# Where the softmax denominators are applied in a fused two-branch attention block: on the gate path, or on the probabilities

## The reference, cut to what matters

```python
m = jnp.maximum(jnp.max(logits, axis=-1, keepdims=True), sk)            # branch A
p = jnp.exp(logits - m)
probs = p / (jnp.sum(p, axis=-1, keepdims=True) + jnp.exp(sk - m))
o = einsum(probs, vb)
probs = jax.nn.softmax(logits, axis=-1)                                 # branch B
...
ya = swa_sink_attention(qa, ka, va, a_sinks[layer]) * jax.nn.silu(za)
yb = chunked_relpos_attention(qb, kb, vb, b_rel_bias[layer]) * jax.nn.silu(zb)
merged = (jax.nn.sigmoid(ga + gate_bias[layer, 0]) * einsum(ya, w_br_a[layer])
          + jax.nn.sigmoid(gb + gate_bias[layer, 1]) * einsum(yb, w_br_b[layer]))
return rms_norm(x + einsum(merged, w_out[layer]), final_g)
```

## Time and profile before

| | |
|---|---|
| median of 3 runs | 3304.91 us (3304.08 to 3306.46) |
| profiled execution: its own time | 3306.4 us |
| profiled execution: span of the trace | 3304.6 us |
| TensorE busy | 3247.2 us (98%) |
| GpSimd, ScalarE, VectorE busy | 1457.4, 1397.8, 1366.8 us (44, 42, 41%) |
| granted TensorE clock | 0.998 of full speed |

### The profile page before, as it was taken

One profiled execution on the slowest core, in us unless ns is written; L12 is line 12 of the kernel. 1 busy time (PEld: TensorE's weight loads), 2 busy tenths in 40 slices (PEclk: granted clock), 3 DMA queues, 4 the chain that ended last, 5 costly groups with the idle time before them and its releaser, 6 DMA issues.

```text
span 3304.6 us, 48009 instructions
## 1 busy us (share of the span) xinstructions
PE 3247.2 (98%) x16248; PEld 2491.4 (75%) x16248; DVE 1366.8 (41%) x2936; ACT 1397.8 (42%) x2929; POOL 1457.4 (44%) x1216
## 2 busy tenths in 40 slices
PE   7999999999999999999999999999999999999998
PEld 6777877778777787777877778777787777877776
DVE  3562345513455134551345513455134551345512
ACT  3543344433444334453344534444344443444432
POOL 5434463344633445334453344533445334553244
PEclk9999999999999999999999999999999999999999
DMA  4222432225322243122431224322253122432123
GB/s 162 66 65 90 172 105 60 65 83 173 107 59 65 87 168 111 59 65 84 168 110 60 64 84 173 105 60 64 86 173 103 60 64 90 172 99 60 58 90 115
DMA packets 100218, 322.25 MB, mean 98 GB/s; under 512 B 11248, under 2 KB 27760, under 8 KB 97776
## 3 DMA queue, kind: packets, MB, share of 16 engines
q1 hardware_dynamic: 99952, 318.90, 29.9%
HBM read 299.45 MB, written 16.78 MB: 96 GB/s over the span
## 4 chain that ended last, share of the span: by engine, by line
PE 92%; DVE 3%; issue 2%; ACT 1%; DMA 1%; POOL 0%; ACTq 0%; SPq 0%; DVEq 0%; POOLq 0%
PE acc L947 16%; PE acc L949 16%; PE acc L948 15%; PE ps_o L1042 6%; PE ps_pt L1011 6%; PE sc L991 4%; PE sc L947 4%; PE sc L949 4%; PE sc L948 4%; PE sc L982 2%; PE sc L891 2%; PE sc L889 2%; PE sc L890 2%; PE sc L914 1%; PE acc L1051 1%
## 5 line engine op out<-in xcount | busy, mean ns | idle before, releaser
L770 POOL TENSOR_TENSOR w_lo<-w_raw,w_hi 128x512 fp32r<-128x512 f32 x928 | 1199.2, 1299 | 1766.2 <-ACT w_hi L1090 1765.4
L947 PE MATMUL acc<-h_hi,w_hi 128*128 128x512 f32 x2432 | 1007.7, 414 | 0.0
L949 PE MATMUL acc<-h_hi,w_lo 128*128 128x512 f32 x2432 | 952.6, 392 | 0.0
L948 PE MATMUL acc<-h_lo,w_hi 128*128 128x512 f32 x2432 | 949.6, 390 | 0.0
L1090 ACT ACTIVATE w_hi<-w_raw 128x512 fp32r<-128x512 f32 x928 | 577.3, 625 | 426.0 <-DMA w_raw<-w 119.5
L947 PEld LDWEIGHTS acc<-h_hi,w_hi 128*128 128x128 f32 x2432 | 457.1, 188 | 130.7 <-issue 56.3
L949 PEld LDWEIGHTS acc<-h_hi,w_lo 128*128 128x128 f32 x2432 | 456.4, 188 | 101.2
L948 PEld LDWEIGHTS acc<-h_lo,w_hi 128*128 128x128 f32 x2432 | 458.8, 189 | 74.5
L1178 ACT ACTIVATE probs_b<-sc,negm 128x640 f32<-128x640 f32 x256 | 203.6, 796 | 372.0 <-DVE negm L1294 371.3
L1185 ACT ACTIVATE probs_t<-ps_pt 128x512 f32<-128x512 f32 (+1 forms) x272 | 154.5, 568 | 333.2 <-PE ps_pt L1011 333.2
L1319 DVE SCALAR_TENSOR_TENSOR part<-th,sc 128x512 f32<-128x512 f32 x64 | 43.9, 686 | 449.1 <-PE sc L949 449.1
(11 more groups left out here) (135 smaller groups left out, 3884.3 us busy)
## 6 DMA issues: line engine op xcount, KB each, us to landing
w_raw<-w SPq DMA_DIRECT2D x464, 512.0 KB, 3.5
rows<-x SPq DMA_DIRECT2D x36, 512.0 KB, 7.7
xt<-x_t SPq DMA_DIRECT2D x16, 1024.0 KB, 9.3
out<-rows SPq DMA_DIRECT2D x32, 512.0 KB, 2.8
x_in<-x SPq DMA_DIRECT2D x28, 512.0 KB, 5.4
cs<-rope_tab SPq DMA_DIRECT2D x8, 512.0 KB, 4.3
rot<-pre SPq DMA_DIRECT2D x160, 16.0 KB
bias<-near SPq DMA_DIRECT2D x1, 1024.0 KB, 13.6
```

What stands on the lines that cost most here:

```text
L770: pool.tensor_tensor(w_lo[n % 2][:, c], w_raw[n % 2][:, c], w_hi[n % 2][:, c].bitcast(FP32), ALU.subtract).then_inc(w_split, 1)
L947: pe.matmul(dst[:, :], hi, src_hi[:, k, :], start=begin, stop=False)
L948: pe.matmul(dst[:, :], hi, src_lo[:, k, :], start=False, stop=False)
L949: mm = pe.matmul(dst[:, :], lo, src_hi[:, k, :], start=False, stop=end)
```

## The change

The denominators move from the gate path to the probabilities.

- A new step `scale` follows each `exps` in the list. GpSimd waits for the exponentials of one query tile (both heads). For an A set it adds exp(sink - max) to the two sums. It raises the sums to the power -1 and multiplies the two tiles of probabilities in place with the result. Turns wait for this (`probs_scaled`) and no longer for the exponentials.
- exp(sink - max) is made by ScalarE one column at a time, just ahead of the exponential of the same head and query tile: 256 instructions in A sets instead of 64.
- `D` and `norm` are gone: no reciprocal and no spreading on DVE, no four transposes and no product `gate` for each of the 64 sets, and no `acc` bank taken for it.
- `ps_o` is cleared by a DVE memset, once a block behind the B values' copies and after each `gate` but the last, and all value matmuls accumulate. The first values of a set wait for the memset (`o_zeroed`) instead of for L1378.
- With no group to start, the turns of B sets come in another order: key tile -3 first, which needs query tiles 0 and 1 alone, then -2, -1, 0, 1, 2 and the last one. The number of transposes and value matmuls and their sizes stay.
- The factor 0.5 moves into `gate` on ScalarE and `gate_rest` on DVE.
- The weight tile `z7` comes two tiles later, and z's tanh uses another buffer.

```diff
-B_TURNS = [[(0, -1)], [(1, -1)], [(0, 0)], [(1, 0)], [(0, -2)], [(1, -2)], [(0, 1)], [(1, 1)],
-           [(0, -3), (1, -3)], [(0, 2), (1, 2)], [(0, -4), (1, -4), (0, 3), (1, 3)]]
+B_TURNS = [[(0, -3), (1, -3)], [(0, -2)], [(1, -2)], [(0, -1)], [(1, -1)], [(0, 0)], [(1, 0)], [(0, 1)],
+           [(1, 1)], [(0, 2), (1, 2)], [(0, -4), (1, -4), (0, 3), (1, 3)]]
-B_BURSTS = [[-1], [0], [-2], [1], [-3], [2], [-4, 3]]
+B_BURSTS = [[-3], [-2], [-1], [0], [1], [2], [-4, 3]]
-B_OUT = (1, 0, 0, 1, 0, 0, 1, 1, 0, 0, 0)
+B_OUT = (1, 0, 0, 1, 0, 0, 1, 0, 0, 1, 0)
...
-A_BEATS = "T0 F G T1 F H D T2 V0 V1 S0 F E0 T3 F F S1 V2 V3 F E1 F S2 F E2 F F S3 F E3 F"
-B_BEATS = "F T0 F G T1 F H D T2 F T3 F V0 V1 S0 S1 T4 F E0 T5 F E1 T6 F T7 F V2 V3 S2 S3 T8 F E2 T9 F T10 E3 F V4 V5 V6"
+A_BEATS = "T0 F G T1 F H T2 V0 V1 S0 F E0 T3 F F S1 V2 V3 F E1 F S2 F E2 F F S3 F E3 F"
+B_BEATS = "F T0 F G T1 F H T2 F T3 F V0 V1 S0 S1 T4 F E0 T5 F E1 T6 F V2 V3 S2 S3 T7 F E2 T8 F T9 E3 F T10 F V4 V5 V6"
...
-        lead[at_] = [("scores", 0, t), *lead[at_], ("exps", 0, t)]
+        lead[at_] = [("scores", 0, t), *lead[at_], ("exps", 0, t), ("scale", 0, t)]
...
-                plan.append(("exps", nxt, no))
+                plan += [("exps", nxt, no), ("scale", nxt, no)]
...
+                    elif step[0] == "scale":
+                        s, t = step[1:]
+                        n, c = POS[s], slice(2 * t, 2 * t + 2)
+                        total = sums[:, n % 2, c]
+                        if s < PAIRS:
+                            hold(sink_exp, b * (2 * TT * PAIRS) + (2 * TT * s + 2 * t + 2))
+                            hold(probs_ready, unit(b, s, t, 1) + 1)
+                            pool.tensor_tensor(total, total, esink[:, c], ALU.add).then_inc(den_ready, 1)
+                            hold(den_ready, b * (TT * PAIRS) + (TT * s + t + 1))
+                        else:
+                            hold(probs_ready, unit(b, s, t, 1) + 1)
+                        pool.tensor_tensor(rden[:, n % 2, c], total, minus[:, :], ALU.pow).then_inc(rden_ready, 1)
+                        hold(rden_ready, tile_no(b, s, t) + 1)
+                        for hh in range(2):
+                            p_ = weights_of(s, hh, t)
+                            pool.tensor_scalar(p_, p_, rden[:, n % 2, 2 * t + hh:2 * t + hh + 1], None,
+                                               ALU.mult).then_inc(probs_scaled, 1)
...
-                pe.wait_ge(probs_ready, unit(b, s, needed - 1, 1) + 1)
+                pe.wait_ge(probs_scaled, unit(b, s, needed - 1, 1) + 1)
...
-                    if not (first and POS[s] == 0):
-                        pe.wait_ge(y_whole, b * SETS + POS[s])
+                    pe.wait_ge(o_zeroed, b * SETS + POS[s] + 1)
...
-                                       start=j == every[0], stop=j == every[-1], skip_group_check=True)
+                                       start=False, stop=j == every[-1], skip_group_check=True)
...
-                    elif kind == "norm":
-                        claim(b, step)
-                        pe.wait_ge(rows_ready, b * SETS + (POS[step[1]] + 1))
-                        turn_four(b, step, part)
...
+                            if s < PAIRS:
+                                head = head_no(s, hh)
+                                act.activation(esink[:, c:c + 1], negm[:, POS[s] % 2, c:c + 1], ACT.Exp,
+                                               bias=sink_sb[:, head:head + 1]).then_inc(sink_exp, 1)
...
-                        wait_freed(dve, b, ("norm", s))
-                        dve.tensor_tensor(whole[:, :], ps_o[:, :], gate[:, :], ALU.mult).then_inc(y_whole, 1)
+                        wait_freed(dve, b, ("job", "z", s))
+                        dve.tensor_tensor(whole[:, :], ps_o[:, :], z[POS[s] % 2][:, :], ALU.mult).then_inc(y_whole, 1)
+                        if s != ORDER[-1]:
+                            dve.wait_ge(y_whole, b * SETS + (POS[s] + 1))
+                            dve.memset(ps_o[:, :], 0.0).then_inc(o_zeroed, 1)
```

More of the change, by code:

```diff
@@ L98, in weight_tiles @@
         tiles += [("ga", d), ("gb", d)]
+        if d == 0:
+            tiles.append(("z", SETS - 1))
     for d in range(KT):
@@ L109 @@
 V_BANK = 1
+Z_TH = 2 * AHEAD - 1
 SQUARED_AT = (4, 5, 8, 10)
@@ L206, in block_plan @@
                     plan.append(("keep_v", ORDER[n - 1]))
-        assert quarters == BEATS_QUARTERS and ("norm", s) in plan
+        assert quarters == BEATS_QUARTERS
     for steps in fill:
@@ L268, in check_plan @@
     assert [step[1] for step in PLAN if step[:1] == ("mm",) and step[2] == 0] == list(range(NW))
-USES_ACC = ("job", "turn_v", "norm")
+USES_ACC = ("job", "turn_v")
 check_plan()
@@ L741, in _ @@
             pool.memset(mhalf[:, :], -0.5).then_inc(zeroed, 1)
+            pool.memset(minus[:, :], -1.0).then_inc(zeroed, 1)
             pool.memset(k_a[:, 0:P], 0.0).then_inc(zeroed, 1)
@@ L1142, in job_done @@
                 elif name == "z":
-                    act.activation(th[:, 0, :], ps, ACT.Tanh, scale=0.5).then_inc(z_tanh, 1)
+                    act.activation(th[:, Z_TH, :], ps, ACT.Tanh, scale=0.5).then_inc(z_tanh, 1)
                 elif name in ("ga", "gb"):
                     i = ("ga", "gb").index(name)
-                    if name == "ga" and idx == 0:
+                    if 2 * idx + i == Z_TH:
                         wait_freed(act, b, ("job", "z", ORDER[-1]))
@@ L1185, in body @@
                             act.activation(ring(first, turn)[:, 0:n], ps_pt[:, 0:n], ACT.Copy).then_inc(pt_out[0], 1)
-                    elif kind == "sink" and step[1] < PAIRS:
-                        s = step[1]
-                        nm = negm[:, POS[s] % 2, :].rearrange("p (t h) -> p h t", h=2)
-                        es = esink[:, :].rearrange("p (t h) -> p h t", h=2)
-                        for hh in range(2):
-                            head = head_no(s, hh)
-                            act.activation(es[:, hh, :], nm[:, hh, :], ACT.Exp,
-                                           bias=sink_sb[:, head:head + 1]).then_inc(sink_exp, 1)
                     elif kind == "gate":
@@ L1198, in body @@
                             act.wait_ge(out_sent, b * (16 * TT))
-                        act.activation(y_hi[:, s, :], whole[:, :], ACT.Copy).then_inc(y_hi_done, 1)
+                        act.activation(y_hi[:, s, :], whole[:, :], ACT.Copy, scale=0.5).then_inc(y_hi_done, 1)
                     elif kind == "next_square" and not last:
@@ L1353, in body @@
                         dve.tensor_copy(v_b[:, TT + 1, :], ps_v[1]).then_inc(v_out[1], 1)
-                    elif kind == "denominators":
-                        s = step[1]
-                        n = POS[s]
-                        dve.wait_ge(probs_ready, unit(b, s, TT - 1, 1) + 1)
-                        total = sums[:, n % 2, :]
-                        if s < PAIRS:
-                            dve.wait_ge(sink_exp, b * (2 * PAIRS) + (2 * s + 2))
-                            dve.tensor_tensor(den[:, :], total, esink[:, :], ALU.add).then_inc(den_ready, 1)
-                            dve.wait_ge(den_ready, b * PAIRS + (s + 1))
-                            total = den[:, :]
-                        dve.reciprocal(rden[:, :], total).then_inc(rden_ready, 1)
-                        dve.wait_ge(rden_ready, b * SETS + (n + 1))
-                        dve.tensor_scalar(part[:, :].rearrange("p (n c) -> p n c", c=HD),
-                                          rden[:, :].unsqueeze(2).to_broadcast([P, 2 * TT, HD]), 0.5, None,
-                                          ALU.mult).then_inc(rows_ready, 1)
-                    elif kind == "norm":
-                        s = step[1]
-                        wait_full(dve, b, step)
-                        dve.tensor_tensor(gate[:, :], bank(step)[:, :], z[POS[s] % 2][:, :],
-                                          ALU.mult).then_inc(free(step), 1)
+                        dve.wait_ge(v_out[0], 2 * (b + 1))
+                        dve.memset(ps_o[:, :], 0.0).then_inc(o_zeroed, 1)
                     elif kind == "gate":
@@ L1387, in body @@
                         dve.wait_ge(y_hi_done, b * SETS + (POS[s] + 1))
-                        dve.tensor_tensor(y_lo[:, s, :], whole[:, :], y_hi[:, s, :].bitcast(FP32),
-                                          ALU.subtract).then_inc(y_done, 1)
+                        dve.scalar_tensor_tensor(out=y_lo[:, s, :], in0=whole[:, :], scalar=0.5,
+                                                 in1=y_hi[:, s, :].bitcast(FP32),
+                                                 op0=ALU.mult, op1=ALU.subtract).then_inc(y_done, 1)
                     elif kind == "add_rows":
```

26 lines of the change are left out of this document (11 added, 15 removed).

## The result

The changed kernel takes 3549.7 us (median of 4 runs, 3547.4 to 3553.3), the kernel before 3305.3 beside it. The ratio is 1.074 (95% interval 1.072 to 1.076): 244 us slower, where 3298 us and a range up to 3330 were forecast.

The account below looks back on a forecast made before the run. The prediction took TensorE, busy 3247.2 of 3304.6 us, as the bound. From the median of 3304.9 it summed -27.5 (norms) + 5 (scores) + 15 (first sets) + 1 (ScalarE) = -6.5: 3298 us, range 3283 to 3330.

Parts of the forecast that it names:

- the price of the multiplication: On GpSimd, each multiplication of a scale: 0.40 us for 256 columns and 0.72 for 640, upper bounds 0.65 and 1.62.
- it fits: GpSimd in the steady sets: with four scales added, busy 22 of 26 us in A sets, 17 of 27 in B.
- 27.5 us from the norms: On TensorE, 64 norms of four transposes go, each costing 0.43 us: 27.5 us saved.
- 5 us for scores: In 32 A sets, scores of query tile 2 wait for exponentials, losing 0.12 to 0.19 us each: 5 us taken.
- The first set: In each block's first set, scales and low parts queue on GpSimd, delaying turns by 1.9 us: 15 us in 8 blocks.
- 2 to 4 us later: GpSimd's low parts in steady sets come 2 to 4 us later, with room in the list; no loss in the sum.
- ScalarE: One-column sink exponentials at 0.2 to 0.25 us, about 40 us more work on ScalarE; 1 us lost, up to 6.
- rival 1: In the first set a scale under 1.7 us costs turns only ScalarE's 0.5 us, 4 us: 3287 us; chance 0.2.
- VectorE: VectorE gets lighter; the new memset of some 0.5 us is hidden, with 4 us to spare before the values.
- Rival 2: GpSimd becomes the bound, multiplying at the two-input rate; first sets and B sets' turns wait: 3377 us; chance 0.25.
- Rival 3: VectorE's `y_lo` and GpSimd hold each other up, 32 us on top: 3330 us; chance 0.1, with late low parts.

Follow-up runs that it names:

- constant-factor run: The changed kernel with a constant factor of 0.125 in place of the column of reciprocals in both multiplications, output not normalised: 3524.6 us (1.067).
- copy run: The changed kernel with each multiplication replaced by a GpSimd copy of the tile onto itself, output not normalised: 3309.4 us (1.0009).
- A tiles alone: The changed kernel with full multiplications of A tiles only, one column multiplied of B tiles: 3343.3 us (1.011).
- B tiles alone: The changed kernel with full multiplications of B tiles only, one column multiplied of A tiles: 3514.1 us (1.064).
- broadcast version: The changed kernel, same result, with each multiplication written as a two-input product with the reciprocal's column broadcast along the row: 3364.6 us (1.018).

## Why the prediction was wrong

**The step that failed is the price of the multiplication**, and in it the choice of bounds. The prediction took 0.40 and 0.72 us from the copy and 0.65 and 1.62 from the subtraction as the upper end. Measured were 0.93 and 1.90. The bounds assumed that an instruction with one large input can't be dearer than one with two. The constant-factor run shows that it is: 2.5 ns a column, as much as the two-input subtraction takes if nothing of its 1299 ns is fixed, and 852 - 256 x 2.5 = 0.2 us on top, with the column of scalars 0.3. The trace of before had no such instruction of size. An upper end from the nearest row was no upper end. Nor was the lower end as firm as it looked. The prediction took the key copy of 512 columns, 613 ns; the value copy of the same size took 607 to 1087 in the same trace:

```profile
L804 POOL COPY v_b<-v_b 128x512 f32<-128x512 f32 x28 | 26.9, 959 | 0.0
```

The copies of the copy run did keep to the lower price.

The Trainium skill (GPSIMD Engine Reference, 4.1 Engine selection) has instructions with one input near line rate. By this trace the rule holds for copies and not for a multiplication by a scalar, which runs slower than a broadcast product with two inputs. The estimate from its section 3.1, 0.38 and 0.96 us, is 0.4 and 0.5 of what was measured. The measurement decides. Its advice to keep elementwise work off GpSimd was right for the B tiles.

**What the price did.** The steady sets were the prediction's "it fits": 22 of 26 us. With the measured pieces a B scale is 0.73 + 0.21 + 3.75 = 4.7 us, and an A set asks GpSimd for 12.3 + 4 x 4.7 = 31 us in 26. The runs order themselves by that sum, 12.3 + 4 x (0.93 + 2m), with m the duration of a B tile's multiplication. The fourth column is the first set's part: what has come up by the second set's first turn against the run without multiplications, in all 8 blocks. It goes mostly by the price of the A tiles (A tiles alone give 53, B tiles alone 17).

| run | m, us | GpSimd's work in an A set of 26 us | first sets, us | time, us |
|---|---|---|---|---|
| none | 0 | 16 | 0 | 3286.9 |
| copy | 0.72 | 22 | 13 | 3309.4 |
| broadcast product | 1.27 | 26 | 30 | 3364.6 |
| constant factor | 1.82 | 31 | 52 | 3524.6 |
| as changed | 1.90 | 31 | 60 | 3549.7 |

Below the edge the steady sets cost little. At it they cost some 50 us, and beyond it what GpSimd falls behind in an A set is paid in the B set behind it, and in part at half clock.

**Point by point.**

- 27.5 us from the norms, less 5 us for scores: right. Without multiplications it is 3286.9 us; the terms -27.5 + 5 + 4 + 1 gave 3287. The loss at the scores was 0.11 us a set, 3.5 us, below the 4 to 6.
- The first set: right in mechanism and, at the copy's price, in size (12 us against 15). At the true price it is some 60 of the 263 us that the multiplications cost, so the smaller part, though it is all that A tiles cost by themselves.
- Low parts "2 to 4 us later" with room for it: wrong. Even at the copy's price TensorE waits 7.1 us for them. The step counted the scales and left out that the key copy and the rotation stand behind the last one; that is 6 of the 11 us between 3298 and the copy run's 3309.4.
- ScalarE: the sink exponential of one column takes 290 ns, as much as that of four, not 0.2 to 0.25. In the first set it shows once the multiplications are gone: the third turn comes 12.84 us after the scores, not 12.47, which is 3 us in 8 blocks, where rival 1 had 4.
- VectorE: lighter, as said, 1303 us; the memset is hidden, and no value matmul waits for it.
- Rival 2 was what happened, in kind. Its time was too low. It said 3377 for 1.62 us (its terms give 3376), and the broadcast version took 3364.6 at 1.27 already. A straight line from there to the constant factor (1.82 us, 3524.6) puts 1.62 near 3466, an estimate. It counted waits of the turns in three A sets of a block; the runs have them in all four, with low parts as the larger share, and the lower clock, which no term told of. It had 0.25, and the range cut it at 3330.
- Rival 3 played no part: the median of `y_lo` fell from the 865 ns of the earlier trace rows to 693, though its longest is 1764, and TensorE waits 6.0 us for it in both traces.

How much of the 244 us is the clock alone was not tried apart. The 60 us above are read from the granted clock and TensorE's busy time.

## What to carry to other kernels

Before work is moved to GpSimd, measure the very instruction in its very form, or take the range wide: forms that compute the same differ by a half (0.61 against 0.93 us, 1.27 against 1.90), and a copy is no model for a multiplication. Add up the helper engine's work for each stage and compare it with the stage's length; the mean over the span (67% here) did not show the 31 us of work in a set of 26. And a queue that also feeds the busiest engine hits it twice when it runs over: by the wait, and by the lower clock behind the wait. The work itself was not wrong to move: with B tiles' multiplications on ScalarE and the first set left on the gate path, the same idea gains 12 us.

## What the runs showed of the hardware that was not expected

- GpSimd, fp32, per column of 128 partitions: copy 0.83 ns, product with a broadcast column 1.7 ns, multiplication by a constant or a column of scalars 2.5 ns, each with 0.2 to 0.3 us fixed (from 256 and 640 columns).
- On GpSimd a power of two columns takes 0.73 us, about as much as a copy of 640 columns.
- ScalarE's exponential of one column took 290 ns (278 to 305), that of four 293.
- TensorE's clock was granted at 0.63 in a stretch in which it was busy for 0.49 of 4 us and at 0.52 in the next, and products started 0.43 us apart instead of 0.23 to 0.24.
